# One sum, one high part and one low part of A22 in place of two halves each, in a two-layer decoder kernel

## The reference, cut to what matters

```python
u = modulate(h, sh_f, sc_f)
y = jnp.square(jax.nn.relu(u @ mlp_w_up[layer])) @ mlp_w_down[layer]
h = layer_norm(DEEPNORM_ALPHA * h + (1 + g_f) * y, ln_g[2 * layer + 1], ln_b[2 * layer + 1])
```

## Time and profile before

| what | value |
|---|---|
| median of 3 runs | 2198.84 us (2197.66 to 2198.94) |
| the profiled execution | 2198.61 us |
| its span | 2196.9 us |
| mean granted clock of TensorE | 0.997 of full speed |
| TensorE matmuls | 2144.9 us, 98% of the span |
| VectorE / ScalarE / GpSimd busy | 65% / 37% / 17% |
| DMA | 84 GB/s in the mean |

### The profile page before, as it was taken

One profiled execution on the slowest core, in us unless ns is written; L12 is line 12 of the kernel. 1 busy time (PEld: TensorE's weight loads), 2 busy tenths in 40 slices (PEclk: granted clock), 3 DMA queues, 4 the chain that ended last, 5 costly groups with the idle time before them and its releaser, 6 DMA issues.

```text
span 2196.9 us, 28310 instructions
## 1 busy us (share of the span) xinstructions
PE 2144.9 (98%) x9984; PEld 1730.2 (79%) x9984; DVE 1419.3 (65%) x2223; ACT 820.0 (37%) x1457; POOL 373.6 (17%) x273
## 2 busy tenths in 40 slices
PE   6999999999999999999999999999999999999998
PEld 5888888878887787788887876677888888888886
DVE  7423656578576676776768566767747547557556
ACT  4201445161224234233347456546222422422432
POOL 0000220010033032130200022321003303303304
PEclk9999999999999999999999999999999999999999
DMA  7434653314413423314122110211211021021021
GB/s 291 142 98 133 117 131 101 105 39 134 130 63 95 125 66 115 113 59 134 48 96 85 43 39 20 78 58 33 64 58 58 21 74 57 20 75 57 19 77 77
DMA packets 52433, 183.96 MB, mean 84 GB/s; under 512 B 7472, under 2 KB 7648, under 8 KB 52352
## 3 DMA queue, kind: packets, MB, share of 16 engines
q1 hardware_dynamic: 44640, 161.50, 22.8%
q0 software_dynamic: 4944, 16.96, 3.6%
q10 hardware_dynamic: 2768, 4.41, 0.5%
HBM read 174.43 MB, written 8.42 MB: 83 GB/s over the span
## 4 chain that ended last, share of the span: by engine, by line
issue 44%; PE 41%; POOL 8%; DVE 3%; ACT 2%; DMA 1%; SPq 1%; POOLq 0%; ACTq 0%; DVEq 0%
PE ps L2054 11%; PE ps L2056 11%; PE ps L2055 11%; POOL whi L678 4%; POOL wlo L678 2%; PE ps L2519 1%; POOL h_blocks L673 1%; PE ps L2549 1%; PE ps L2533 1%; DMA resid<-in_xt 1%; PE ps L2157 1%; PE ps L2298 1%; PE ps L2283 1%; PE ps L2287 1%; DVE stats L1572 0%
## 5 line engine op out<-in xcount | busy, mean ns | idle before, releaser
L2054 PE MATMUL ps<-uhi,whi 128*128 128x512 f32 x1152 | 451.6, 392 | 11.3 <-DVE wlo L1700 5.0
L2055 PE MATMUL ps<-ulo,whi 128*128 128x512 f32 x1152 | 448.4, 389 | 0.0
L2056 PE MATMUL ps<-uhi,wlo 128*128 128x512 f32 x1152 | 448.3, 389 | 0.0
L2054 PE MATMUL ps<-whi,uhi 128*128 128x512 f32 x704 | 288.2, 409 | 2.4 <-ACT resid L1111 2.2
L2056 PE MATMUL ps<-whi,ulo 128*128 128x512 f32 x704 | 276.1, 392 | 0.0
L2055 PE MATMUL ps<-wlo,uhi 128*128 128x512 f32 x704 | 275.4, 391 | 0.0
L2054 PEld LDWEIGHTS ps<-uhi,whi 128*128 128x128 f32 x1152 | 216.2, 188 | 65.2 <-issue 7.3
L1740 DVE TENSOR_TENSOR resid<-ps,resid 128x512 f32<-128x512 f32 x336 | 217.9, 680 | 54.8 <-PE ps L2056 53.7
L2056 PEld LDWEIGHTS ps<-uhi,wlo 128*128 128x128 f32 x1152 | 216.3, 188 | 45.3
L2055 PEld LDWEIGHTS ps<-ulo,whi 128*128 128x128 f32 x1152 | 216.3, 188 | 44.0
L1021 ACT ACTIVATE h_blocks<-ps 128x512 f32<-128x512 f32 x96 | 57.2, 596 | 516.5 <-PE ps L2056 516.5
(11 more groups left out here) (300 smaller groups left out, 3542.1 us busy)
## 6 DMA issues: line engine op xcount, KB each, us to landing
stage<-in_stream SPq DMA_DIRECT2D x276, 512.0 KB, 3.6
aux<-in_early SPq DMA_DIRECT2D x8, 512.0 KB, 7.1
early_place<-in_early SPq DMA_DIRECT2D x8, 512.0 KB, 14.2
resid<-in_xt SPq DMA_DIRECT2D x8, 512.0 KB, 15.9
resid<-in_x POOLq DMA_DIRECT2D x8, 512.0 KB, 9.5
resid_dram<-resid ACTq DMA_DIRECT2D x8, 512.0 KB, 2.6
resid<-resid_dram POOLq DMA_DIRECT2D x8, 512.0 KB, 3.6
out<-resid SPq DMA_DIRECT2D x7, 512.0 KB, 2.6
```

The lines of the kernel that those rows point to most:

```text
L2054: pe.matmul(dst, left_hi, right_hi, start=start, stop=False, skip_group_check=more)
L2055: pe.matmul(dst, left_hi, right_lo, start=False, stop=False, skip_group_check=more)
L2056: return pe.matmul(dst, left_lo, right_hi, start=False, stop=stop, skip_group_check=more)
```

## The change

In each seven-product chunk the work on A22 that was done in two halves, the first behind up group 6 and the second behind up group 7, is done in one piece behind up group 7. The sum `h_block(6)` on VectorE, the high part of `h_block(3)` on ScalarE and its low part on VectorE become one operation each of 128 x 1024 in place of two of 128 x 512. Each counts its semaphore by two, so that all other waits stay as they are.

```diff
@@ ScalarE, seven_up @@
-                    if u >= 6:
-                        act.wait_ge(h_sums, 4 * q0 + u - 4 + 4 * i)
-                        high(h_part(2)[:, u - 6, :], h_block(3)[:, u - 6, :])
+                act.wait_ge(h_sums, 4 * q0 + 3 + 4 * i)
+                act.activation(h_part(2), h_block(3), ACT.Copy).then_inc(operand_hi, 2)
                 done("P7")
@@ VectorE, seven_chunk @@
-                def half_sum(f):
-
-                    v.wait_ge(h_squared, 8 * q0 + 7 + f + 8 * i)
-                    v.tensor_tensor(h_block(6)[:, f, :], h_block(2)[:, f, :], h_block(3)[:, f, :],
-                                    ALU.add).then_inc(h_sums, 1)
-
-                def half_low(f):
-
-                    v.wait_ge(operand_hi, 15 * q0 + 4 + f + 15 * i)
-                    v.tensor_tensor(h_part(3)[:, f, :], h_block(3)[:, f, :], fr(h_part(2)[:, f, :]),
-                                    ALU.subtract).then_inc(h_low, 1)
-
...
-                half_sum(0)
-                half_low(0)
-                half_sum(1)
-                half_low(1)
+                v.wait_ge(h_squared, 8 * q0 + 8 + 8 * i)
+                v.tensor_tensor(h_block(6), h_block(2), h_block(3), ALU.add).then_inc(h_sums, 2)
+                v.wait_ge(operand_hi, 15 * q0 + 5 + 15 * i)
+                v.tensor_tensor(h_part(3), h_block(3), fr(h_part(2)), ALU.subtract).then_inc(h_low, 2)
                 add("P7", 0, 1, 2)
```

## The result

The changed kernel takes 2250.32 us in the median of 4 runs (2249.93 to 2251.18), against 2198.88 for the kernel before: a ratio of 1.0233, 95% interval 1.0217 to 1.0248. That is 51.4 us, 4.29 in each of the twelve seven-product chunks, where the prediction had 0.95. The range ended at 2213. Two single executions of the later series, one of the kernel before at 4365.7 us and one of before_weight_first at 7728.9 us, lie far outside the rest, and the ratios leave them out.

What follows compares the result with a forecast made beforehand. TensorE was taken as the bound, with a matmul in flight for 98% of the span; P2 starting 0.95 us late a chunk, 12 x 0.95 = 11.4 on 2198.61, gave 2210.0 us, range 2198.0 to 2213.0.

Steps and rivals of the forecast that it cites:

- What bounds the kernel now: TensorE, busy 98% of the span; each chunk loses 0.46 us at P2, waiting for VectorE's low_of(4, 1, 6).
- What leaves and what comes: Merged halves save 0.33 us a chunk on VectorE and 0.21 on ScalarE, counted at nothing since neither engine is the bound.
- The chain behind the eighth up group: Sum, high part and low part after that group take 0.53, 0.42 and 0.52 us longer; low part ends at 610.15.
- together 1.48: Growth in us of the serial sum, high part and low part, from 1218 - 690, 1056 - 633 and 1216 - 692 ns.
- The turn at 612.7: VectorE's h_block(8) subtraction begins just ahead of GpSimd's first L678, which then ends at 616.18 in place of 615.23.
- the other outcome: VectorE goes first, GpSimd's first L678 waits, and P2 starts 0.95 us a chunk late: 2210.0 us; chance 0.74.
- a lead of 0.15 us: How far VectorE's subtraction for h_block(8), at 612.67, was expected to begin ahead of GpSimd's first L678, at 612.82.
- Rival (a): GpSimd's first L678 goes ahead of VectorE's h_block(8); P2 is 3.36 us a chunk late, 2238.9 us; chance 0.14.
- P4's start: P4 waits for VectorE's low part and first P7 add, starting at 610.88 in place of 610.53, inside P2's present wait.

Runs made afterwards that it cites:

- before_weight_first: Kernel before, with ScalarE behind the end of P7 copying the weight's high part ahead of that of h_block(1); 2194.5 us, ratio 0.9975.
- unit_counts: Changed kernel with the three merged operations counting their semaphores by one and the waits renumbered; 2210.0 us, ratio 1.0048 to the kernel before.
- unit_weight_first: unit_counts with ScalarE behind the end of P7 copying the weight's high part ahead of that of h_block(1); 2249.21 us, ratio 1.0223 to the kernel before.
- low_whole: Kernel before with only the low part of A22 merged (count by two), sum and high part in halves; 2200.49 us, ratio 0.9999.

## Why the prediction was wrong

It named direction, place and both outcomes, and picked the wrong one of the two. Point by point:

- *What bounds the kernel now* held: P2 waits for `low_of(4, 1, 6)` behind GpSimd's first L678. Two experiments took that wait away, by VectorE's order and by ScalarE's, and each gained 5 us of the 5.5 possible.
- *What leaves and what comes* held. The saved busy time bought nothing.
- *The chain behind the eighth up group* is **the step that failed**. The term "together 1.48" was mis-sized: 1.70 was measured. It took the three hand-overs as unchanged and noted that the semaphores count by two without asking what that costs: three waits became rows of their own, 0.07 us each. With counts of one the chain grew by 1.50.
- *The turn at 612.7* therefore fell the other way. The working for the other outcome was right: in unit_counts P2 begins 12.10 after the eighth Relu (618.15 against 606.05) where it was 11.15, 0.95 as forecast, and the median rose by 10.2 us where 11.4 was forecast. But a lead of 0.15 us on a sum of six terms was given 0.74 against 0.14, because the twelve chunks repeat to 0.01 us. Repeatability of a trace says how well the old program is known; it says nothing about terms that the new program adds.
- *Rival (a)* was what happened, priced at 3.36 a chunk in place of 4.29. Up to P2 it was right: P2 begins 14.48 behind the eighth Relu (620.00 against 605.52), where the rival's 619.80 against 605.29 is 14.51. It lacked P2's fourth tile. With three PSUM banks that tile takes the bank of P2's first tile and waits until VectorE has added it; the add (624.48 in the timeline above) stands behind `low_of(5, 0, 8)`, which with the shifted turns takes 2.96. That wait is the 1.01 at 625.21.
- *P4's start* was given as 0.35 late and measured as 0.49. The counts by two are 0.20 of that, since it is 0.29 late in unit_counts (611.58 with the Relu at 606.05, against 610.53 and 605.29). The other way, the hand-over from VectorE to TensorE, taken as 0.13 from P2's wait, was 0.06 from the add to the matmul. As predicted, P4's late start is not what costs where VectorE has the turn.
- The range followed from the chances: with a step of 30 us at a distance of 0.15 us, it should have reached across the step.

The Trainium skill, page "SBUF — State Buffer", section "Who interferes with whom", gives the rule that issue order decides who blocks. The pair unit_counts and unit_weight_first agrees: the same three operations and the same waits for them, L1760 at 1.23 or at 3.42 us by which of the two engines was ready first. That the pair is held for the whole instruction, which the prediction took from there, the section writes of VectorE's 2-port modes; for two SBUF inputs it says only that they contend, and it is the rows of this case that show whole turns.

## What to carry to other kernels

Where two engines take turns at a shared resource, look for the place at which their requests come close together, and expect a step in the cost of a delay there, and not only a slope (here 0.85 a chunk just below it and 4.29 just above): work out both outcomes, and set the range over both unless the lead is larger than all hand-overs in the chain together. Here, where neither engine is the bound, a serial chain across two engines was better left in halves: merging saved 0.54 us of busy time a chunk and made the chain 1.50 longer. And count a semaphore by one where the operation also has to wait; renumber the waits rather than keep them by counting two.

## What the runs showed of the hardware

- An operation that waits and counts by two gets its wait as a separate EVENT_SEMAPHORE row (21 ns on VectorE, 17 ns on ScalarE in the queue) and starts 0.06 to 0.07 us later after the releaser's end than the same operation with a count of one (0.09 to 0.11 against 0.03 to 0.04), on both engines. low_whole, with one such operation, shows one such row and one such gap: high part until 609.77, low part from 609.87.
- GpSimd going on to an operation whose operand is ready is recorded from 0.03 us before its former one's end (613.06 against 613.09), while VectorE, released by that same end, is recorded from 0.03 after it. With GpSimd's operand ready VectorE did not win at that place in any of the twelve chunks of the changed kernel or of unit_weight_first; it won when GpSimd had to wait 0.17 us (unit_counts). No run lies between the two.
- Once decided, the turns repeat to 0.01 us over all twelve chunks: no chunk of the changed kernel fell the other way.
